# Interleaving the rounded weights of two contraction tiles: stationary loads that read every second column

## The reference, cut to what matters

```python
proj = u @ w_in[l]                                  # 1024 x 6152
mix = jnp.concatenate([h, y], axis=-1) @ w_out[l]   # 2048 x 1024
up = causal_dwconv(u @ ffn_up[l], ffn_conv_w[l], ffn_conv_b[l])   # 1024 x 5632
f = (jax.nn.silu(gt) * a) @ ffn_down[l]             # 2816 x 1024
proj = jnp.einsum('bsd,de->bse', h, w_in)           # attention: 3088 columns, recurrence: 4096
gate, up = jnp.split(jnp.einsum('bsd,df->bsf', h, w_in), 2, axis=-1)
```

## Time and profile before

| | us |
|---|---|
| median of 3 runs | 2200.99 (2195.91 to 2202.62) |
| profiled execution, whole | 2200.18 |
| profiled execution, span | 2198.1 |
| TensorE matmuls busy | 2138.4 (97%) |
| TensorE weight loads busy | 1709.5 (78%) |
| GpSimd busy | 1498.2 (68%) |
| VectorE busy | 1117.0 (51%) |
| ScalarE busy | 663.2 (30%) |

### The profile page before, as it was taken

The page is one execution under the profiler, slowest core; times in us unless marked ns, Lnnn a source line. Parts: engine busy times, 40 slices in busy tenths (PEclk is TensorE's granted clock), DMA queues, the critical chain, the costliest instruction groups (busy, mean ns, idle before and its releaser), DMA issues.

```text
span 2198.1 us, 26833 instructions
## 1 busy us (share of the span) xinstructions
PE 2138.4 (97%) x9588; PEld 1709.5 (78%) x9588; DVE 1117.0 (51%) x1982; ACT 663.2 (30%) x1142; POOL 1498.2 (68%) x741
## 2 busy tenths in 40 slices
PE   7999999999999999999999999999999999999997
PEld 3878777768888887788868888886788777888886
DVE  6899974884444103777643222105877835222101
ACT  3413335123222103444442111104555534111100
POOL 5868575667777887644379777886333348877785
PEclk9999999999999999999999999999999999999999
DMA  6323223732333332222123333332222222333332
GB/s 247 107 84 96 77 78 106 268 142 96 95 95 96 105 105 86 80 84 78 48 76 106 96 97 99 102 106 83 59 67 68 68 68 77 96 96 98 102 105 86
DMA packets 56371, 215.98 MB, mean 98 GB/s; under 512 B 6216, under 2 KB 6216, under 8 KB 53088
## 3 DMA queue, kind: packets, MB, share of 16 engines
q1 hardware_dynamic: 52992, 206.96, 29.3%
q10 hardware_dynamic: 3296, 7.91, 1.1%
HBM read 212.70 MB, written 2.15 MB: 98 GB/s over the span
## 4 chain that ended last, share of the span: by engine, by line
PE 78%; DVE 10%; POOL 4%; ACT 3%; issue 3%; DMA 2%; SPq 0%; DVEq 0%; POOLq 0%; ACTq 0%
PE ps L371 63%; DVE y L2036 3%; PE ps L603 2%; PE ps L1192 2%; DMA raw<-in_wstream 2%; PE ps L408 2%; POOL w_hi L974 1%; POOL w_lo L980 1%; PE ps L1284 1%; PE ps L1130 1%; PE ps L1315 1%; PE ps L1421 1%; PE ps L1302 1%; ACT u_hi L476 1%; DVE u_lo L526 1%
## 5 line engine op out<-in xcount | busy, mean ns | idle before, releaser
L980 POOL TENSOR_TENSOR w_lo<-raw,w_hi 128x1024 fp32r<-128x1024 f32 x335 | 813.6, 2429 | 199.3 <-ACT w_hi L1879 175.5
L974 POOL TENSOR_TENSOR w_hi<-raw,ones 128x1024 fp32r<-128x1024 f32 x304 | 582.9, 1918 | 368.9 <-DMA raw<-in_wstream 368.3
L371 PE MATMUL ps<-u_hi,w_hi 128*128 128x512 f32 x1760 | 708.9, 403 | 7.1 <-DVE qk L2047 2.8
L371 PE MATMUL ps<-u_hi,w_lo 128*128 128x512 f32 x1760 | 687.9, 391 | 0.0
L371 PE MATMUL ps<-u_lo,w_hi 128*128 128x512 f32 x1760 | 686.5, 390 | 0.0
L371 PEld LDWEIGHTS ps<-u_hi,w_hi 128*128 128x128 f32 x1760 | 332.1, 189 | 77.2 <-issue 6.7
L371 PEld LDWEIGHTS ps<-u_hi,w_lo 128*128 128x128 f32 x1760 | 331.1, 188 | 71.2
L371 PEld LDWEIGHTS ps<-u_lo,w_hi 128*128 128x128 f32 x1760 | 331.9, 189 | 66.9 <-issue 3.6
L371 PE MATMUL ps<-f_hi,w_lo 128*128 128x512 f32 x528 | 205.4, 389 | 0.0
L371 PE MATMUL ps<-f_hi,w_hi 128*128 128x512 f32 x528 | 205.4, 389 | 0.0
L371 PE MATMUL ps<-f_lo,w_hi 128*128 128x512 f32 x528 | 205.4, 389 | 0.0
(11 more groups left out here) (366 smaller groups left out, 2901.4 us busy)
## 6 DMA issues: line engine op xcount, KB each, us to landing
raw<-in_wstream SPq DMA_DIRECT2D x342, 512.0 KB, 3.6
ada_buf<-in_ada SPq DMA_DIRECT2D x16, 1024.0 KB, 7.3
ada_start<-in_ada SPq DMA_DIRECT2D x8, 1024.0 KB, 17.0
cbc<-decay_rows ACTq DMA_DIRECT2D x7, 512.0 KB, 3.5
x<-in_xT SPq DMA_DIRECT2D x1, 2048.0 KB, 8.0
bc<-gate_rows ACTq DMA_DIRECT2D x4, 512.0 KB, 5.3
out_T<-x ACTq DMA_DIRECT2D x8, 256.0 KB, 2.2
prm<-in_params SPq DMA_DIRECT2D x1, 357.5 KB, 2.9
```

Source lines behind the costliest of these rows:

```text
L371: last = nc.tensor.matmul(out, a, b, start=(start and k == 0 and i == 0), stop=(stop and k == nk - 1 and i == 2))
L974: g.tensor_tensor(w_hi[slot][:], raw[slot][:], ones[:, 0:1].to_broadcast([P, D]), ALU.mult).then_inc(chunk_hi, 1)
L980: g.tensor_tensor(w_lo[slot][:], raw[slot][:], w_hi[slot][:].bitcast(f32), ALU.subtract).then_inc(chunk_split, 1)
```

## The change

The high weights of two neighbouring contraction tiles `k` (even) and `k + 1` are written interleaved into the 256 columns that both take: column `i` of the even tile to place `2i`, column `i` of the odd one to `2i + 1`. A pass reads its 128 high weights at every second column, from place 0 or 1 of the pair. Low weights keep their places. The three functions that write or read `w_hi` on GpSimd and ScalarE get patterns with three free dimensions (pairs, tile of the pair, column), and every reader of high weights goes through `high_of`.

```diff
+    def high_of(slot, k):
+        return w_hi[slot][:, k // 2 * 2 * P + k % 2:(k // 2 + 1) * 2 * P:2]
+
+    def low_of(slot, k):
+        return w_lo[slot][:, k * P:(k + 1) * P]
+
+    def by_pairs(t, cols=slice(0, D)):
+        return t[:, cols].rearrange("p (j s i) -> p j s i", s=2, i=P)
+
+    def interleaved(t, cols=slice(0, D)):
+        return t[:, cols].rearrange("p (j i s) -> p j s i", s=2, i=P)
...
-            wh, wl = w_hi[slot][:, k * P:(k + 1) * P], w_lo[slot][:, k * P:(k + 1) * P]
+            wh, wl = high_of(slot, k), low_of(slot, k)
...
+        def one_by_pairs(n):
+            return ones[:, 0:1].to_broadcast([P, n]).rearrange("p (j s i) -> p j s i", s=2, i=P)
+
         def split(c, slot, landed, rounded):
 
             pool.wait_ge(raw_landed[slot], landed)
-            g.tensor_tensor(w_hi[slot][:], raw[slot][:], ones[:, 0:1].to_broadcast([P, D]),
+            g.tensor_tensor(interleaved(w_hi[slot]), by_pairs(raw[slot]), one_by_pairs(D),
                             ALU.mult).then_inc(chunk_hi, 1)
             low(c, slot, chunk_hi, rounded)
 
         def low(c, slot, sem_, rounded):
             pool.wait_ge(sem_, rounded)
-            g.tensor_tensor(w_lo[slot][:], raw[slot][:], w_hi[slot][:].bitcast(f32),
+            g.tensor_tensor(by_pairs(w_lo[slot]), by_pairs(raw[slot]), interleaved(w_hi[slot]).bitcast(f32),
                             ALU.subtract).then_inc(chunk_split, 1)
...
-            A(w_hi[c % SLOTS][:], raw[c % SLOTS][:], ACT.Identity).then_inc(chunk_hi_act, 1)
+            A(interleaved(w_hi[c % SLOTS]), by_pairs(raw[c % SLOTS]), ACT.Identity).then_inc(chunk_hi_act, 1)
```

More of the change, by code:

```diff
@@ L390, in gemm_first @@
         for k in range(KT):
-            weights = [[w[(chunk + g) % SLOTS][:, k * P:(k + 1) * P] for w in (w_hi, w_lo)] for g in range(GROUP)]
+            weights = [[of((chunk + g) % SLOTS, k) for of in (high_of, low_of)] for g in range(GROUP)]
             high_wait(k)
@@ L624, in finish @@
             k = KT - 1
-            weights = [[w[(self.base + n) % SLOTS][:, k * P:(k + 1) * P] for w in (w_hi, w_lo)] for n in range(self.width)]
+            weights = [[of((self.base + n) % SLOTS, k) for of in (high_of, low_of)] for n in range(self.width)]
             if self.kept:
@@ L998, in split_halves @@
                 cols = slice(h * D // 2, (h + 1) * D // 2)
-                high = g.tensor_tensor(w_hi[slot][:, cols], raw[slot][:, cols], ones[:, 0:1].to_broadcast([P, D // 2]), ALU.mult)
+                high = g.tensor_tensor(interleaved(w_hi[slot], cols), by_pairs(raw[slot], cols), one_by_pairs(D // 2), ALU.mult)
                 if h == 0:
@@ L1005, in split_halves @@
                     pool.wait_ge(chunk_hi, c + 1 - taken(c))
-                rest = g.tensor_tensor(w_lo[slot][:, cols], raw[slot][:, cols], w_hi[slot][:, cols].bitcast(f32), ALU.subtract)
+                rest = g.tensor_tensor(by_pairs(w_lo[slot], cols), by_pairs(raw[slot], cols), interleaved(w_hi[slot], cols).bitcast(f32), ALU.subtract)
                 if h == 0:
@@ L1189, in wout_pe @@
                 hi, lo = (y_hi, y_lo) if half else (u_hi, u_lo)
-                wh, wl = w_hi[c % SLOTS][:, k * P:(k + 1) * P], w_lo[c % SLOTS][:, k * P:(k + 1) * P]
+                wh, wl = high_of(c % SLOTS, k), low_of(c % SLOTS, k)
                 for i, (a, b) in enumerate(tri(wh, wl, hi[:, k, :], lo[:, k, :])):
@@ L1791, in _ @@
                     act.wait_ge(chunk_split, C_FOXOUT + 1)
-                    for j, w in enumerate((w_hi, w_lo)):
-                        ins = A(last_row[:, j, :], w[C_FOXOUT % SLOTS][:, (KT - 1) * P:KT * P].bitcast(f32), ACT.Identity)
+                    for j, of in enumerate((high_of, low_of)):
+                        ins = A(last_row[:, j, :], of(C_FOXOUT % SLOTS, KT - 1).bitcast(f32), ACT.Identity)
                     a_fg.did(ins, "last_row")
```

## The result

| | before | after |
|---|---|---|
| median, us (4 runs each) | 2199.38 (2195.91 to 2202.62) | 2234.73 (2230.65 to 2237.22) |
| ratio, 95% interval | | 1.0159 (1.0136 to 1.0182) |
| span of the profiled execution, us | 2198.1 | 2232.4 |

The changed kernel is slower by 34 to 35 us. The time lies inside the range on record, but the forecast case (no change, 2201) did not happen, and none of the rivals did. The lines moved with the change: L371 is now L383, L974 is L989, L980 is L995, L999 is L1014, L1879 is L1894. The span's granted clock is 0.994 in both.

A forecast was written before the change was run, and what follows sets the result against it. TensorE's passes of 226.7 ns were taken to set the time, with GpSimd behind them having least room. Four terms summed 0 + 0 + 0 + 0 = 0, so the forecast was 2201 us, range 2193 to 2260 (0.80).

The forecast's parts named there:

- the forecast case: Whole kernel: all four changed access patterns cost zero, time 2201 us, 2198 to 2204 for this case; chance 0.54.
- rivals A and B: GpSimd and ScalarE: strided writing dear, 2210 to 2227 (0.16); reading too, GpSimd becomes the bound, 2249 to 2266 (0.12).
- term 1: TensorE's strided high-weight loads, about 5370: zero, hidden by the 226.7 ns pass; three times the price would be 88 ns late.
- Rival C: TensorE's passes: the load beside slows them and the step ends that, 226.7 to 215 ns, 2152 us; chance 0.12.
- The rule on 16-byte lines: SBUF needs two hits in a 16-byte line for full bandwidth; columns 8 bytes apart give two, so all four places cost zero.
- Terms 2 to 4: GpSimd's strided rounding writes, GpSimd's subtraction with one strided input, ScalarE's 31 strided roundings: each taken as zero.
- the four durations: Signs: passes 226.7 ns, GpSimd's rounding 1896 and subtraction 2401, ScalarE's rounding 1057; room 120 ns a load, 0.55 us GpSimd's pair.

The follow-up runs named there:

- the experiment: Kernel before with TensorE alone reading the high weights at every fourth column, 16 bytes apart; 2255.54 us, ratio 1.0259.

## Where the prediction was right, and where wrong

**The forecast case did not hold.** 2201 was forecast, 2234.7 came. The range to 2260 held the time, but for the sake of rivals A and B, which were about a slower GpSimd and ScalarE, and the kernel with only their part of the change ran at 1.0006 of the time before. That the number lies in the range is luck: a number inside a range by another mechanism confirms nothing of its steps.

**The step that failed is term 1,** the loads at "zero: hidden, by the pass". What the sentence says is true of the long pieces: a load's +6.7 ns is covered, and so is +121 ns in the experiment's first piece. The fault is what it took the price of a load to be. It asked only how long the load is and whether a pass covers it, with a bound at 226.7 ns and a room of 120 ns. Even that room was read off too generously: it takes the load at 105 ns, the distance in a row of one-column passes, while the earlier trace rows has loads of 189 ns beside a pass, which leaves 38. But the length was not what mattered. The price came by another way: a pass next to loads of another address pattern starts 4.4 to 6.7 ns later, 26.2 us in the three long pieces, and the kernel that differs from before in these loads alone has the whole loss (2234.86 us). The Trainium skill, TensorE: Matmul & The Clock Gate, section Step-by-step: what each phase is for, says what the term relied on without naming it: loading the next tile's weights takes no read bandwidth from the running matmul. The moved loads (226.7 to 231.1 ns with no change in their duration) show that the two aren't independent here, whatever the path is.

**Rival C named the right place with the wrong sign,** and the row against it was too weak. It let the load disturb the pass, but only so that the change would end it. Its estimate of 215 ns for an undisturbed pass was never reached: 226.7 is the shortest mean of a 512-column pass in any kernel here. And the argument from the earlier trace rows, 0.42 us to ScalarE's start with and without a load beside the pass, compares two ends in units of 10 ns for one pair, both in order. The same place in the kernel after:

```profile
818.35 0.39 PE L383 MATMUL ps<-f_hi,w_lo 128*128 128x512 f32 x1
...
818.78 0.60 ACT L668 ACTIVATE sq<-ps 128x512 f32<-128x512 f32 x1 [14.31 <-PE ps L383]
```

A chunk's last pass starts, with a load beside it, and releases ScalarE 0.43 us later: the view that was chosen to exclude a disturbance hardly shows the one that is there. The distance from start to start over 1512 passes, shows it to a hundredth of a nanosecond. Beside the load's duration the term should have carried a price per pass, bounded on both sides: no row of before showed any pass with another pattern beside it, so a few nanoseconds, times 5370 or times all 9588, could not be excluded.

**The rule on 16-byte lines** (the Trainium skill, SBUF — State Buffer, section Specifications (TRN2)) fits the load's own record: two hits in a line, 195 ns against 188; one hit, 309. It doesn't give the time: both steps give a pace of 233.3 ns in the first piece, and a load in order, 4 bytes beside its tile, loses 4.4 ns a pass. So the sum by that rule was zero, as mine, and failed with it.

**Terms 2 to 4 held.** GpSimd's rounding: zero taken, up to +0.50 us kept, -2 ns measured; the reason, that reading sets its pace, agrees with that. Its subtraction: zero taken, at most +0.505 us, +35 ns measured (+29 with writing alone). The Trainium skill's threshold of more than 8 bytes (GPSIMD Engine Reference, section Performance pitfalls for Q7 kernels) agrees with this so far: at exactly 8 bytes the price is 35 ns of 2401; no run here reads with a wider step on GpSimd. ScalarE: between zero and +1.06 us, +94 ns measured, 3 us of work in all, of which the kernel that only writes with the step shows nothing on the time (0.9996 to 1.0016). Line 2547, with VectorE's doubled price for writing, was not the right neighbour for either engine.

**What was to show it** was named rightly: the chain's piece of 1512 passes, expected at 343 us, reads 352.80, while the four durations stayed far within the room that the last paragraph gave them (7 of 120 ns for a load). That list of durations as the only way to be wrong was the same mistake as in term 1.

**What stays open.** Why the pace depends on the places. Shown are: in the first piece the load's duration makes no difference (195 or 309 ns), a step is not needed for the loss, reading the fewest places doesn't avoid it, GpSimd and ScalarE have no part in it, and the places of the load and of the activations matter. Also open is what makes one and the same pattern run at 231.1 ns in one stretch and at 233.3 in another. Other places for the whole of `w_hi`, `w_lo`, `u_hi` and `f_hi` were not tried, so whether 226.7 is the least is open too. None of the kernels that do the same work was faster than the one before.

## What to carry to other kernels

When a stretch is nothing but one engine's instructions, read the distance from start to start, not the durations of what lies beside them, and multiply each doubtful nanosecond by the count: 6.7 ns by 1512 made 10 us, in rows where every load was "hidden". A change of layout for an operand that TensorE reads needs its own price per pass, bounded on both sides, even if its load is covered twice. One long chain of equal passes is a scale fine enough to test such a layout by itself, one stage to one setting, in a single run, if each setting stands in several stages: one pattern ran at two paces here.

## What the runs showed of the hardware that was not expected

- With 512 activation columns the pace is 226.7 ns if loads and activations are in order at their tile's start; every other setting tried gave 228.8 to 235.6, except the load moved by 16 bytes (226.8). In triples of passes the first pieces of the kernels with one setting gave 680, 686.6, 693.3 and 700 ns.
- The changed kernel held 231.1 ns a pass through one feed-forward network and 233.3 through the next, with the same tiles, slots and read pattern.
- A pass of 508 columns took longer (227.7 ns, one stretch) than one of 512.
- A weight load's record can be longer than the distance of passes (309 ns against 233.3) without slowing them in a long piece, and its own pass then starts 70 to 80 ns before the record ends.
- GpSimd writes 1024 rounded values at every second place as fast as in order (1894 against 1896 ns); ScalarE takes 9% longer for it (1151 against 1057 ns).
